# A transformer layer with 32 experts on one core: normed rows in natural order, expert biases added on VectorE, a smaller first index step, one more tile opened to weights early

## What is computed

```python
x = x + g1 * (merged @ w_out)                       # 512 x 1024
h2 = rms_norm(x, norm2_g) * (1.0 + sc2) + sh2       # "normed rows"
logits = h2 @ w_router + b_router                   # 32 experts, the best 4 of each token
for each expert e, on the tokens that chose it:
    gu = xb @ w_gu[e] + b_gu[e]                     # 1024 -> 2 * 512
    gt, up = gu[:, :512], gu[:, 512:]
    gt = min(gt, 7.0);  up = clip(up, -7.0, 7.0)
    act = gt * sigmoid(1.702 * gt) * (up + 1.0)
    y += weight * (act @ w_down[e] + b_down[e])     # 512 -> 1024
out = rms_norm(x + g2 * y)
```

## Time and profile before

| | before |
|---|---|
| median of 3 runs | 937.23 us (936.38 to 937.92) |
| the profiled execution, its own time | 932.74 us |
| its span, first to last instruction | 931.0 us |
| mean granted clock of TensorE | 0.994 |
| PE busy | 895.7 us (96%) |
| DVE busy | 454.4 us (49%) |
| ACT, POOL busy | 180.2 us, 250.0 us |
| DMA | 283.75 MB, mean 305 GB/s |

### The profile page before, as it was taken

How to read it: one execution, slowest core, us unless ns; L and a number is a source line. 1 busy time by engine, 2 the same in 40 slices (tenths; PEclk the granted TensorE clock), 3 DMA queues, 4 the chain that set the end, 5 groups by cost and what they waited for, 6 DMA issues and landing times.

```text
span 931.0 us, 22683 instructions
## 1 busy us (share of the span) xinstructions
PE 895.7 (96%) x10115; PEld 525.3 (56%) x10115; DVE 454.4 (49%) x946; ACT 180.2 (19%) x361; POOL 250.0 (27%) x248
## 2 busy tenths in 40 slices
PE   3999999999999998989999999999999999999994
PEld 2676756766788755755545454544545454544551
DVE  0389967544633556754352534344352534344355
ACT  6344454544322414100000000000000000000012
POOL 2333952202400003223223131323223131323102
PEclk9999999999999999999999999999999999999998
DMA  9937554305422967679999999999999999999965
GB/s 322 366 130 271 181 173 157 123 1 198 175 96 79 408 259 293 257 301 354 375 407 390 407 399 402 404 399 407 394 409 395 409 397 407 404 402 408 391 246 195
DMA packets 64124, 283.75 MB, mean 305 GB/s; under 512 B 7428, under 2 KB 9052, under 8 KB 39448
## 3 DMA queue, kind: packets, MB, share of 16 engines
q1 hardware_dynamic: 53528, 257.93, 69.8%
q0 software_dynamic: 10496, 24.32, 9.3%
HBM read 271.83 MB, written 18.50 MB: 312 GB/s over the span
## 4 chain that ended last, share of the span: by engine, by line
PE 84%; DVE 9%; ACT 3%; DMA 2%; issue 1%; SPq 0%; DVEq 0%; ACTq 0%; POOLq 0%
PE ps L1859 36%; PE ps L1578 16%; PE ps L1882 12%; PE ps L1872 6%; PE ps L1813 2%; DVE small L1157 2%; DVE top L1156 2%; PE ps L1632 2%; PE ps L1718 2%; PE ps L1853 2%; PE ps L1599 1%; DMA moe_rows<-X 1%; PE ps L1733 1%; DVE small L1142 1%; DMA X<-in_x_dram 1%
## 5 line engine op out<-in xcount | busy, mean ns | idle before, releaser
L1354 DVE TENSOR_SCALAR mix<-ps 128x384 f32<-128x384 f32 x32 | 17.9, 558 | 280.1 <-ACT attn L1019 280.1
L753 POOL DMA_INDIRECT moe_rows<-mix,idx x31 | 45.9, 1482 | 345.6 <-DVE mix L1412 345.6
L1578 PE MATMUL ps<-h_hi,wb_hl 128*128 128x512 f32 x384 | 125.5, 400 | 0.0
L1019 ACT ACTIVATE attn<-ps 128x384 f32<-128x384 f32 x32 | 15.7, 491 | 493.2 <-PE ps L1859 493.2
L747 POOL DMA_INDIRECT apad<-h_rows,idx x93 | 97.3, 1046 | 50.6 <-issue 27.7
L1578 PEld LDWEIGHTS ps<-h_hi,wb_hl 128*128 128x128 f32 x384 | 72.1, 188 | 20.8 <-issue 3.9
L1859 PE MATMUL ps<-ring,mix 128*32 128x256 f32 x1440 | 80.0, 379 | 0.0
L1859 PE MATMUL ps<-ring,uvp 128*32 128x256 f32 x1344 | 76.3, 383 | 0.0
L1578 PE MATMUL ps<-h_lo,wb_hl 128*128 128x512 f32 x192 | 74.8, 390 | 0.0
L1404 DVE SCALAR_TENSOR_TENSOR mix<-ps,WC,attn 32x256 f32<-32x256 f32 x128 | 61.6, 481 | 3.8 <-PE ps L1872 1.4
L1859 PEld LDWEIGHTS ps<-ring,mix 128*32 128x32 f32 x1440 | 43.0, 110 | 33.1
(11 more groups left out here) (312 smaller groups left out, 1346.7 us busy)
## 6 DMA issues: line engine op xcount, KB each, us to landing
ring<-in_w_gu_dram SPq DMA_DIRECT2D x58, 1024.0 KB, 23.8
ring<-in_w_down_dram SPq DMA_DIRECT2D x30, 1024.0 KB, 25.7
ring<-in_w_ada_dram SPq DMA_DIRECT2D x12, 2048.0 KB, 11.2
area_b<-in_w_gu_dram SPq DMA_DIRECT2D x17, 1024.0 KB, 18.9
hT<-in_w_gu_dram SPq DMA_DIRECT2D x17, 1024.0 KB, 22.9
area_a<-in_w_gu_dram SPq DMA_DIRECT2D x15, 1024.0 KB, 23.7
X<-in_w_gu_dram SPq DMA_DIRECT2D x14, 1024.0 KB, 26.1
ring<-in_w_in_dram SPq DMA_DIRECT2D x6, 2048.0 KB, 9.1
```

The costliest lines, as they stand in the source:

```text
L753: pool.indirect_dma_start(out=y_dram, in_=Y[0:slots, b, :], in_offset=None, out_offset=bass.IndirectOffsetOnAxis(ap=which, axis=0), bounds ...
L1578: last = mm(out_, a, b, start=(n == 0 and start_), stop=(n == len(pairs) - 1))
```

## The change

It has four parts.

1. **Normed rows in natural order.** `h2[ch]` is no longer regrouped: DVE adds contiguous rows. PE (transposes and the matmuls for expert 0) and POOL (the staging copy) now read them through the view `h2_block`, with a step of 8 elements (32 bytes). `h2[2]` moves from `X` to `uvp`, so chunk 2 no longer waits for `y_begun[2]`. For chunks 2 and 3 the scaled row is written where the result goes. `first` moves from `uvp` to `mix`. The temporary of `x1_half` moves from `small` to `apad`.
2. **Biases on VectorE.** `b_gu` comes in four DMAs, one operation on POOL and one DVE transpose at the start of DVE's part make `bias_cols`; for each expert one DVE transpose (`bias_rows`) spreads its column to a row `brow`, and one `tensor_tensor` of 128x768 (`biased`) adds it while copying gates and ups out of PSUM. The 12 bias matmuls of each expert, `sel3` and the operations on POOL that split the bias go. The sigmoid and `activate` read `biased` from SBUF. The next `up` waits for `biased_ok` and no longer for `av_ok`.
3. **Own index step for experts 1 to 3.** `quarter_rows` is done for group 0 alone, and then for group 1. `places(0)` stands inside the loop for expert 0's rows, behind k = 5. On DVE `rows(1)` stands before `gated(0)`, and `one_hot(2)` before the second `quarter_rows`.
4. **The tile `small` open to weights.** It is now the home of piece 12 instead of 14, and is loaded once the last `A` job is added and `row_out` is there; pieces 13 and 14 take the two halves of the last ring slot.

```diff
-        h2 = [X[:, ch, :] for ch in range(C - 1)] + [apad_flat[:, PG * (PAD + T) - D:PG * (PAD + T)]]
+        h2 = [X[:, 0, :], X[:, 1, :], uvp[:, :, :].rearrange("p a t -> p (a t)"),
+              apad_flat[:, PG * (PAD + T) - D:PG * (PAD + T)]]
+        h2_block = [t.rearrange("p (q k) -> p k q", k=KD) for t in h2]
...
-        homes = ([t[:, i * PAIR:(i + 1) * PAIR] for t in pairs for i in range(2)] + [small[:, :], latent[:, :]]
+        homes = ([t[:, i * PAIR:(i + 1) * PAIR] for t in pairs for i in range(2)] + [latent[:, :]]
                  + [last_pair[:, i * PAIR:(i + 1) * PAIR] for i in range(2)])
-        kept = [i for i in range(PRE) if i != 2 * len(pairs)]
+        homes.insert(12, small[:, :])
+        kept = [i for i in range(PRE) if i != 12]
...
+            sp.wait_ge(by_vec, emptied[number["A", KD - 1]])
+            sp.wait_ge(row_out, 32)
+            load_up(2, 2, 12)
             used(NFP - 1)
-            load_up(2, 2, 12)
             load_up(2, 3, 13)
-            sp.wait_ge(by_vec, emptied[number["out", 2 * C - 1]])
             load_down(1, 0, 14)
...
                 nc.gpsimd.tensor_copy(staged[ch % 2].rearrange("p (a k f) -> p k a f", a=NQ, k=KD),
-                                      h2[ch].rearrange("p (k a f) -> p k a f", a=NQ, k=KD)).then_inc(staged_ok, 1)
+                                      h2[ch].rearrange("p (a f k) -> p k a f", a=NQ, k=KD)).then_inc(staged_ok, 1)
...
-                if e == OHE * 2:
-                    pool.wait_ge(idx_ok, 2)
+                if e in (OHE, OHE * 2):
+                    pool.wait_ge(idx_ok, 1 + e // OHE)
...
-                act.wait_ge(half_used, up_no(e, 3) + 1)
-                nc.scalar.activation(th, gates, ACT.Sigmoid, scale=ALPHA).then_inc(th_ok, 1)
+                act.wait_ge(biased_ok, e + 1)
+                nc.scalar.activation(th, gate_in, ACT.Sigmoid, scale=ALPHA).then_inc(th_ok, 1)
...
-                link(v.scalar_tensor_tensor(out=natural, in0=X[:, ch, :], scalar=rstd3[:, ch:ch + 1], in1=A2b,
+                scaled = natural if ch < 2 else h2[ch]
+                if ch == C - 1:
+                    dve.wait_ge(xg_clear, 1)
+                link(v.scalar_tensor_tensor(out=scaled, in0=X[:, ch, :], scalar=rstd3[:, ch:ch + 1], in1=A2b,
                                             op0=ALU.mult, op1=ALU.mult))
-                if ch < C - 1:
+                if ch < 2:
                     dve.wait_ge(y_begun[ch], 16)
-                else:
-                    dve.wait_ge(xg_clear, 1)
-                v.tensor_tensor(h2[ch].rearrange("p (k q) -> p k q", k=KD), by_k(natural), by_k(sh2b),
-                                ALU.add).then_inc(h2_ok, 1)
+                v.tensor_tensor(h2[ch], scaled, sh2b, ALU.add).then_inc(h2_ok, 1)
...
+            def bias_rows(cols, done):
+
+                v.transpose(brow.rearrange("p (m f) -> p m f", m=8),
+                            cols.rearrange("p (m s) -> p m s", s=1).broadcast_to([P, 8, SB])).then_inc(done, 1)
...
                 dve.wait_ge(*up_done)
+                v.tensor_tensor(biased, ps[:, 0:SG, 0:2 * P], brow.rearrange("p (g n) -> p g n", g=1)
+                                .broadcast_to([P, SG, 2 * P]), ALU.add).then_inc(with_bias, 1)
...
-            dve.wait_ge(rep_ok, 1)
-            quarter_rows(0, 2 * OHE)
-            for g in (2, 3, *LATE_GROUPS[0]):
+            one_hot(2)
+            dve.wait_ge(rep_ok, 2)
+            quarter_rows(5, OHE, OHE)
+            for g in (3, *LATE_GROUPS[0]):
                 one_hot(g)
+            rows(1)
             gated(0)
-            rows(1)
...
-                for g in range(SG):
-                    for j in range(4):
-                        mm(ps[SB * j:SB * (j + 1), g, 0:2 * P], bias.broadcast_to([3 * NE, SB]), b3_of[:, j, :, :],
-                           start=True, stop=False, tile_position=(0, SB * j))
...
-                    last = mm(ps[:, 4 + k // 4, (k % 4) * P:(k % 4) * P + slots], h2[ch][:, k * P:(k + 1) * P], first[:, ch, :],
+                    last = mm(ps[:, 4 + k // 4, (k % 4) * P:(k % 4) * P + slots], h2_block[ch][:, k, :], first[:, ch, :],
                               start=(ch == 0), stop=(ch == C - 1))
+                if k == 5:
+                    places(0)
             last.then_inc(tx_done, 1)
-            places(0)
+            quarter_rows(3, 0, OHE)
             start("ix", 1)
             places(1)
```

More of the change, by code:

```diff
@@ L627, in _ @@
                                              base=-part * NE, pattern=[[-1, NE]], channel_multiplier=1))
-            link(nc.gpsimd.memset(sel3[:, :], 0.0))
-            for part in range(3):
-                link(nc.gpsimd.affine_select(out=sel3[:, :], in_=sel3[:, :], compare_op=ALU.not_equal, fill=1.0,
-                                             base=-part * NE, pattern=[[-1, NE]], channel_multiplier=1))
             for g in range(PG):
@@ L1790, in h2_turn @@
                     for k in range(4):
-                        at = (4 * half + k) * P
-                        last = nc.tensor.transpose(b_[:, k * P:(k + 1) * P], h2[ch][:, at:at + P], ident[:, :])
+                        last = nc.tensor.transpose(b_[:, k * P:(k + 1) * P], h2_block[ch][:, 4 * half + k, :], ident[:, :])
                     last.then_inc(job_done, 1)
@@ L1847, in _, with up_all @@
             chain(b_[:, C * NE:(C + 1) * NE], [(onesb[:, :], maskh[:, k, :]) for k in range(C)], job_done)
[L1849 to L1854 removed]
+            def up_all(b, arrived, done, between={}):
                 for k in range(KD):
```

122 lines of the change are left out of this document (61 added, 61 removed).

## The result

The changed kernel takes 944.48 us (median of 7 runs, 942.20 to 947.41), the kernel before 936.84 beside it (7 runs, 934.65 to 937.92). The ratio is 1.0088, with an interval of 1.0069 to 1.0107: 7.6 us slower, where 7.6 us faster was forecast. The profiled execution took 942.98 us, with a span of 941.3. That is 10.2 us more than the profiled one of before (932.74), which was shorter than all seven runs of that kernel, so the rows differ by more than the medians do.

A forecast was written before the change was run, and what follows sets the result against it. PE sets the pace, with the slower DMA weight stream 1.3 us from limiting; the stream's start moves both. Front 2.1, expert 1 4.2 and reserve 1.3 make 7.6 us off 937.23: 929.6 us, range 927 to 941.

The forecast's parts named there:

- T: Time of one PE read of 128 strided columns in the changed kernel; taken as unchanged, chance 0.38.
- its port has a factor of 2 in hand here: PE's float32 reads: 0.45 ns a column in the fast form against 0.90 for `h2`, so the step was taken as free.
- The bound from VectorE, 0.256: Upper end for T: DVE's 2.0 ns per strided column times 128 columns, a cost of 13.0 us.
- my formula: Cost of PE's strided reads before and in expert 0: 64 (T - 0.115) + 32 (T - 0.108) - 0.7 us.
- The other term, 32 transposes: PE's 32 transposes of the normed rows: cost 32 (T - 0.108) us, less 0.7 us covered by ACT's copies.
- rival 3: A strided column costs PE what it costs DVE, 2.0 ns: cost 13.0 us, kernel at 942.6 us; chance 0.17.
- The front: Chain up to the square of chunk 3: 2.3 + 0.2 - 0.4 = 2.1 us earlier, between 0 and 2.5.
- The tile's push on the save: Piece 12, loaded at about 333 us, shares the engines with the save of chunk 0: 0.4 us added.
- at worst: The save of chunk 0 waits for the whole of piece 12: 2.6 us at 400 GB/s.
- Expert 1: Before `up(1)`: idle wait 2.46, slow stretch 1.5 and bias 0.44 us go, less small costs: a lead of 4.2 us.
- The biases and the stream: 29 experts lose 0.44 us each, 12.8 us of PE's time; 1.3 us shows, the rest becomes waits for pieces.
- The reserve of 1.3 us: At the last `down`, the last piece lands 1.3 us before PE needs it; a faster PE alone gains that.

The follow-up runs named there:

- the kernel with the step alone: The kernel before, with only expert 0's 64 row matmuls reading their blocks with a step of 8 elements; 1.0103 of the kernel before, with stops.
- The old place: The changed kernel with piece 12 in its former place and the former order of loads; 1.0055 of the kernel before without stops, 0.9957 with stops.
- both undone: The changed kernel with rows regrouped by VectorE and piece 12 in its former place; 0.9946 of the kernel before without stops, 0.9845 with stops.
- The lightened kernel before: The kernel before with 24 matmuls (an eighth of the products) left out of each `up`, all pieces still loaded; 0.9940 of the kernel before, without stops.

## Why the prediction was wrong

**T, the open price: the step that failed.** "I take T unchanged" was wrong: T is 0.238 to 0.245 us in the matmuls. The working behind it ("its port has a factor of 2 in hand here", taken from 0.45 against 0.90 ns a column) did not carry: it set the 512 moving columns of one matmul against a record that reads 128 stationary and 96 moving columns, and neither row had a step in it. A step of 4 elements costs a factor of 2 outright (0.231 against 0.110 us). The bound from VectorE, 0.256, was almost the answer, and the rule of the Trainium skill that I cited against this part (page "SBUF — State Buffer", section "Door 1: The DMA port swizzle") named the condition rightly. By my formula with T = 0.24 the row matmuls cost 8.0 us; measured 8.3 (11.75 + 3.94 - 7.38), and 8.2 in the kernel with the step alone. The other term, 32 transposes, was to be priced by the same T and is nearly free (0.11 to 0.12 us). So that rival 3's time, 942.6, lay close to the result is luck: it charged the transposes and a little too much for a read, and left out what follows.

**The clock.** No case had the slow reads take the granted clock down. Half clock from 382 to 399 us stretched `places(0)` and the start of `up(0)`; the strided reads kept their pace (0.239 us a record). The first load that waits for a used piece is issued 13.3 us late (400.73 instead of 387.45), of which 2.2 is the front and 8.3 the reads. The remaining 2.8 us are the half clock: the matmuls of `places(0)` and `places(1)` ahead of the weights take 1.21 + 1.37 instead of 1.40 us, and from the first weights to that load it is 4.46 (from 396.27) instead of 2.87 us (from 384.58). The index step put ahead of `up(0)` costs 0.43 us and the bias gone there gives back 0.44.

**The front.** Forecast 2.1 us earlier, measured 2.2 later. The contiguous additions give what was said (0.82 us each) and the wait for chunk 2's save is gone. The tile's push on the save was taken at 0.4 us and was 2.95 between the two traces, 2.0 against the average of the traces without the early piece; that is near my "at worst" of 2.6 and not near 0.4. The old place gives 3 us back. "POOL's copies are used much later and cost nothing" was wrong in another way than through their users: while GpSimd copies, VectorE's scaling all but stands, and it grew by 0.93 to 1.04 us for each of two chunks.

**Expert 1.** Right in size: 13.3 us late at the first load, 8.6 at `up(2)`, so 4.7 us of lead against 4.2 forecast, and with these two parts alone in the kernel 4.5 us at `up(2)` and 5.1 us in the time (0.9946), against the 5.5 of their terms. But it is not the index step's gain: that alone gives 2.4 us at `up(2)`, the rest only together with the biases on VectorE. The next wait of `up(1)`, for the gates to be read out of PSUM, is hidden in the changed kernel as forecast, since the addition ends it early; with the index step alone it is 1.02 us.

**The biases and the stream.** Right: the last piece lands 484.5 us behind the start of `up(2)` before, 484.4 after and 483.8 in the version with both undone. PE's waits came in the last experts, seven of them from 777.26 to 879.51 us in that version, 17.04 us apart (17.0 forecast). The addition takes 0.96 us and the bias transpose 0.40 (1.0 and 0.4 forecast). An expert is 15.81 us, not 15.67: `up` itself grew from 10.36 to 10.50 without the bias ahead of it. The reserve of 1.3 us brought nothing here: PE ends the last `down` 5.8 us behind the last landing in the kernel before, 6.9 in the changed one and 6.9 with both undone. The lightened kernel before gained 4.8 us by the medians, of which its trace shows 1.4 ahead of `up(2)`; where the rest comes from is open. Waits before the last `down` take PE's lead and more: behind each of the two long ones the changed kernel ran at half clock, and `down`'s wide part took 5.28 instead of 3.58 us.

## What to carry to other kernels

An open price of an access pattern that stands on the path should be bounded by the far end and not decided by an argument on headroom: one kernel with only the pattern changed settles it. When a piece is loaded earlier, look which transfer on the path is under way and add the whole piece to it, not its share; and when an operation off the path grows, look at what runs beside it, not only at who uses its result. Where a stream sets the end, a shorter inner loop pays next to nothing, and what moves the first uses moves the end (8.6 us at `up(2)` and 7.6 in the time; 4.5 and 5.1); where PE sets the pace, as with stops, the same shorter loop gave 9.7 us.

## What the runs showed of the hardware

- A float32 matmul whose stationary or moving operand of 128 columns has a step of 16 or 32 bytes takes 0.23 to 0.24 us a record, against 0.11 to 0.12 at 4 or 8 bytes, and the strided record takes 0.24 us at 2.4 as at 1.2 GHz; a transpose takes 0.11 us at 4 and at 32 bytes.
- With some 15.6 us of such reads (in the changed kernel with 1.2 us of other matmuls among them) the granted clock fell from 2.4 to 1.2 GHz while they ran, though PE was busy throughout: 17 us at half in each of the six traces that have them, and in none of the others. In groups of 3.7 us with bfloat16 filling between (0.7 us from its start to the next group's) it did not.
- GpSimd's copy of 128x1024 float32 takes 1.05 us contiguous and 2.04 to 2.14 with a step of 8 elements on the input side, and a scaling with two full inputs on VectorE made next to no progress beside it (2.2 to 2.3 us instead of 1.28).
- The same kernel takes 936 or 969 to 974 us, the latter with stops of 0.4 to 0.6 us in PE's weight loads in each `up`. What causes them is open.
